# The causal mask of the forgetting attention: from a TensorE matmul to the added row of sums

## The reference

```python
def block(args):
    qi, ci, pi = args
    s = jnp.einsum('bqhd,bkhd->bhqk', qi, k).astype(jnp.float32) * scale
    s = s + ci.transpose(0, 2, 1)[..., None] - cum_k
    mask = kpos[None, :] <= pi[:, None]
    s = jnp.where(mask[None, None], s, NEG_INF)
    p = jax.nn.softmax(s, axis=-1).astype(v.dtype)
    return jnp.einsum('bhqk,bkhd->bqhd', p, v)
```

## Time and profile before

| | us |
|---|---|
| median of 3 runs | 2692.89 |
| lowest and highest | 2692.72, 2695.39 |
| the profiled execution | 2693.89 |
| its span in the profile | 2692.2 |
| TensorE matmuls, busy | 2624.7 (97%) |
| VectorE, busy | 1806.2 (67%) |
| ScalarE, busy | 1130.0 (42%) |
| steps of the forgetting attention | from 1360.5 to about 1977 |

### The profile page before, as it was taken

One profiled execution on the slowest core, in us unless ns is written; L12 is line 12 of the kernel. 1 busy time (PEld: TensorE's weight loads), 2 busy tenths in 40 slices (PEclk: granted clock), 3 DMA queues, 4 the chain that ended last, 5 costly groups with the idle time before them and its releaser, 6 DMA issues.

```text
span 2692.2 us, 39002 instructions
## 1 busy us (share of the span) xinstructions
PE 2624.7 (97%) x12209; PEld 2156.0 (80%) x12209; DVE 1806.2 (67%) x2975; ACT 1130.0 (42%) x2079; POOL 229.9 (9%) x273
## 2 busy tenths in 40 slices
PE   5999999999999999999989999999999999999998
PEld 3688887787888888888868888888878888888886
DVE  7766668785668888888876666666685455644446
ACT  6433336333335555555554444444453322334220
POOL 0000000112120000000001111111100000014100
PEclk9999999999999999999999999999999999999999
DMA  9556864567664444444555545445485455456642
GB/s 359 182 199 204 234 190 122 135 167 163 163 141 119 116 119 116 120 122 123 186 141 130 114 116 130 111 109 108 111 237 159 149 181 184 155 157 195 202 149 101
DMA packets 324800, 418.53 MB, mean 155 GB/s; under 512 B 20392, under 2 KB 223208, under 8 KB 321008
## 3 DMA queue, kind: packets, MB, share of 16 engines
q1 hardware_dynamic: 282048, 343.04, 40.6%
q0 software_dynamic: 29616, 66.12, 13.3%
q10 hardware_dynamic: 13056, 8.39, 1.1%
HBM read 297.90 MB, written 119.59 MB: 155 GB/s over the span
## 4 chain that ended last, share of the span: by engine, by line
PE 87%; DVE 5%; DMA 3%; ACT 3%; issue 2%; SPq 1%; ACTq 0%; DVEq 0%
PE pA L1863 18%; PE pC L1863 18%; PE pD L1863 17%; PE yP L2555 12%; PE zP L2611 11%; PE tP L1765 2%; PE zP L2630 2%; PE sP L2018 2%; PE oP L2041 1%; DMA b_lo<-b_scratch 1%; PE sP L1831 1%; DVE w_lo L1286 1%; DMA w_raw<-in_w_in_dram 1%; PE oP L2043 1%; PE sP L1960 1%
## 5 line engine op out<-in xcount | busy, mean ns | idle before, releaser
L1286 DVE TENSOR_TENSOR w_lo<-w_sum,w_hi 128x512 fp32r<-128x512 f32 x336 | 229.6, 688 | 167.5 <-ACT w_hi L858 166.3
L1863 PE MATMUL pC<-b_hi,w_hi 128*128 128x512 f32 x784 | 308.8, 394 | 6.2 <-DVE b_lo L1260 3.6
L1863 PE MATMUL pA<-b_hi,w_hi 128*128 128x512 f32 x784 | 308.3, 393 | 3.6 <-ACT ctile L874 1.3
L1863 PE MATMUL pD<-b_hi,w_hi 128*128 128x512 f32 x784 | 307.5, 392 | 2.4 <-DVE b_lo L1482 1.3
L1863 PE MATMUL pC<-b_hi,w_lo 128*128 128x512 f32 x784 | 307.1, 392 | 0.0
L1863 PE MATMUL pA<-b_hi,w_lo 128*128 128x512 f32 x784 | 306.9, 392 | 0.0
L1863 PE MATMUL pA<-b_lo,w_hi 128*128 128x512 f32 x784 | 306.7, 391 | 0.0
L1863 PE MATMUL pD<-b_hi,w_lo 128*128 128x512 f32 x784 | 306.1, 390 | 0.0
L1863 PE MATMUL pC<-b_lo,w_hi 128*128 128x512 f32 x784 | 306.1, 390 | 0.0
L1863 PE MATMUL pD<-b_lo,w_hi 128*128 128x512 f32 x784 | 306.0, 390 | 0.0
L180 ACT CAST w_hi<-w_raw 128x1024 fp32r<-128x1024 f32 x122 | 128.5, 1054 | 354.0 <-PE zP L2611 175.2
(11 more groups left out here) (303 smaller groups left out, 5098.6 us busy)
## 6 DMA issues: line engine op xcount, KB each, us to landing
w_raw<-in_w_in_dram SPq DMA_DIRECT2D x168, 512.0 KB, 5.8
proj_scratch<-ctile SPq DMA_DIRECT2D x168, 256.0 KB, 2.2
proj_scratch<-ctile POOLq DMA_DIRECT2D x168, 256.0 KB, 6.0
bg_raw<-in_w_ada_dram SPq DMA_DIRECT2D x64, 512.0 KB, 4.6
w_raw<-in_w_out_dram SPq DMA_DIRECT2D x58, 512.0 KB, 4.0
w_raw<-in_w_br_swa_dram SPq DMA_DIRECT2D x32, 512.0 KB, 4.1
w_raw<-in_w_br_fox_dram SPq DMA_DIRECT2D x32, 512.0 KB, 3.9
aux<-proj_scratch SPq DMA_DIRECT2D x64, 256.0 KB, 4.0
```

The source lines that it names most:

```text
L1286: nc.vector.tensor_tensor(ring(k, True), factor(k), ring(k, False).bitcast(F32), ALU.subtract).then_inc(in_lo, 1)
L1863: last = nc.tensor.matmul(bank(r, k)[:], w[:, j, :], b[:, j, :], start=(k < 4 and n == 0), stop=(n == 11), skip_group_check=True)
```

## The change

The mask matmul and its two constant operands `ident_r` and `mask_r` are dropped. The constant mask stays as float32 (`mask_f`). Before the minimum of step i, VectorE adds the mask to block i of `c_cols`, so that the row that is added to the scores holds the mask. From step i + 1 on that block has to be free of it: ScalarE keeps a copy of each block in `c_kept` before VectorE changes it, and puts it back behind the exponential of the step. A new semaphore `c_block` orders the two: odd values for a kept block, even ones for a masked one. ScalarE instead of VectorE now waits for the load of `c_cols`. Two semaphores of the start, `c_one` and `c_padded`, become one, `c_ready`. The diff, cut to its core:

```diff
@@ main_gpsimd
                 own(nc.gpsimd.memset(mask_f[:], 0.0))
-                own(nc.gpsimd.affine_select(out=mask_f[:], in_=mask_f[:], compare_op=ALU.is_ge,
-                                            fill=-NEG, base=0, pattern=[[-1, P]], channel_multiplier=1))
-                own(nc.gpsimd.tensor_copy(mask_r[:], mask_f[:]))
-                pool.wait_ge(ident_ready, 1)
-                nc.gpsimd.tensor_copy(ident_r[:], ident[:]).then_inc(consts, 1)
+                nc.gpsimd.affine_select(out=mask_f[:], in_=mask_f[:], compare_op=ALU.is_ge, fill=-NEG, base=0,
+                                        pattern=[[-1, P]], channel_multiplier=1).then_inc(consts, 1)
@@ main_scalar, head
+                    def keep(i):
+                        nc.scalar.copy(c_kept[:, i % 2, :], c_cols[:, i * P:(i + 1) * P]).then_inc(c_block, 1)
+
+                    act.wait_ge(c_cols_loaded, 16 * h + 16)
+                    keep(0)
                     for i in range(8):
                         if i < 7:
                             q_high(i + 1)
                         exponentials(i)
+                        if i < 7:
+                            nc.scalar.copy(c_cols[:, i * P:(i + 1) * P], c_kept[:, i % 2, :])
+                            keep(i + 1)
@@ main_vector, head
                     for i in range(8):
+                        diagonal = c_cols[:, i * P:(i + 1) * P]
+                        dve.wait_ge(c_block, 16 * h + (2 * i + 1))
+                        nc.vector.tensor_tensor(diagonal, diagonal, mask_f[:], ALU.add).then_inc(c_block, 1)
+                        dve.wait_ge(c_block, 16 * h + (2 * i + 2))
                         dve.wait_ge(f_qk, 8 * h + (i + 2))
-                        if i == 0:
-                            dve.wait_ge(c_cols_loaded, 16 * h + 16)
@@ main_tensor, scores
                                 last = nc.tensor.matmul(dst, fq[:], fk[:, c0:c1], start=(part == 0), stop=(part == 2))
-                                if part == 0 and a == i // 4:
-                                    nc.tensor.matmul(sP[:, a, (i % 4) * P:(i % 4 + 1) * P], ident_r[:], mask_r[:],
-                                                     start=False, stop=False)
```

More of the change, by code:

```diff
@@ L274, in build @@
             ident = sb("ident", [P, P], F32, main)
-            ident_r = sb("ident_r", [P, P], F32R, main)
-            mask_r = sb("mask_r", [P, P], F32R, main)
+            mask_f = sb("mask_f", [P, P], F32, main)
             c_cols = sb("c_cols", [P, SEQ], F32, main)
@@ L299, in build @@
                     sm = sb("sm", [P, 4, 5], F32, s00)
-                    mask_f = sb("mask_f", [P, P], F32, s00)
                 with ExitStack() as s01:
@@ L342, in build @@
                 fo_st = sb("fo_st", [P, 2, P], F32, s3)
+                c_kept = sb("c_kept", [P, 2, P], F32, s3)
             og_in = [sem(f"og_in_{q}") for q in range(5)]
@@ L352, in build @@
             xh_copied = sem("xh_copied")
-            c_one = sem("c_one")
-            c_padded = sem("c_padded")
+            c_ready = sem("c_ready")
+            c_block = sem("c_block")
             c_loaded = sem("c_loaded")
@@ L1202, in main_vector @@
                 nc.vector.memset(halves[P // 2:P, 1:2], 1.0)
-                nc.vector.memset(c_sb[:, KD:KD + 1], 1.0).then_inc(c_one, 1)
+                nc.vector.memset(c_sb[:, KD:KD + 1], 1.0).then_inc(c_ready, 1)
                 def x_stat(t):
@@ L1405, in main_vector @@
                 dve.wait_ge(c_loaded, 32)
-                nc.vector.tensor_copy(c_pad[:, :, 0], c_sb[:, 0:KD]).then_inc(c_padded, 1)
+                nc.vector.tensor_copy(c_pad[:, :, 0], c_sb[:, 0:KD]).then_inc(c_ready, 1)
                 dve.wait_ge(ada_b_ready, 1)
@@ L1770, in main_tensor @@
                                     ).then_inc(ada_b_turned, 1)
-                pe.wait_ge(c_one, 1)
+                pe.wait_ge(c_ready, 1)
                 def turn_x(t):
@@ L1789, in ada_multiply @@
                         pe.wait_ge(xt_copied, 16)
-                    pe.wait_ge(c_padded, 1)
+                    pe.wait_ge(c_ready, 2)
                     pe.wait_ge(ada_loaded[slot], 32 * (r // 4 + 1))
```

## The result

The changed kernel takes **2708.8 us** (median of 6 runs, 2707.4 to 2711.2) against 2693.4 of the kernel before on the same chip (2692.6 to 2695.4). The ratio is 1.0055, with a 95% interval of 1.0046 to 1.0065: **15.4 us slower**. The forecast was 2699, with a range up to 2703; the time lies outside.

The account below looks back on a forecast made before the run. TensorE was taken to set the pace, with no engine having slack around step 5. Terms -7.0 + 7.2 + 3.2 + 2.4 + 0.3 = +6.1 us gave 2699 us from the median 2692.89, range 2693 to 2703.

Parts of the forecast that it names:

- rival (d): ScalarE's copies don't overlap: 0.19 x 8 at step 5, +1.5 us, 2700.5; chance 0.17 together with Rival (c).
- The matmuls' 0.11: TensorE: each of 64 removed mask matmuls saves its 0.11 us step, 7.0 us in all.
- Added to VectorE: 64 additions of 128x128 ahead of the maxima put each maximum 0.35 to 0.40 us later, taken as 0.36.
- The w_raw load: Heads 1 to 6: additions of steps 2 and 3 delay the next weights' load; +3.2 us, between nothing and 6.3.
- 0.3 for the last: Last head: behind step 7, ScalarE's output projection work hangs on the last maximum, and one mask is lost; +0.3 us.
- Rival (c): The clock falls in head 0 as its wait grows to 2.8 us: +1.6, 2701; chance 0.17 together with rival (d).
- Head 0: Additions and copies delay VectorE's already late weights at steps 1 and 2, and the load; +2.4 us.
- 0.9 of step 5: Step 5, each head: 0.79 us more wait for the copy of pC plus 0.11 for its mask matmul; +7.2 over eight.
- Rival (a): The load lands by itself and is no wait, so 3.2 and 0.6 drop out: +2.3 us, 2695; chance 0.30.
- (b): ScalarE and VectorE have room, so TensorE just gets shorter: -7.0 us, 2686; chance 0.03.

Follow-up runs that it names:

- both_kept: Kernel before with its mask matmuls kept, plus VectorE operations of the addition's size and the change's two ScalarE copies per step; 2705.1 us against 2693.8.
- adds_23: nomask with VectorE's addition of zeros back in steps 2 and 3 of each head alone; 2695.1 us against 2694.0 of the kernel before.
- adds_5: nomask with VectorE's addition of zeros back in step 5 of each head alone; 2695.9 us against 2694.0 of the kernel before.
- nomask_copies: nomask with the ScalarE copies back and no additions; 2692.9 us against 2694.0 of the kernel before.
- adds_rest: nomask with VectorE's addition of zeros back in steps 0, 1, 4, 6 and 7 of each head; 2690.5 us against 2694.0 of the kernel before.
- nomask: Changed kernel without its 64 additions and 120 ScalarE copies, mask matmuls out too, so no causal mask; 2688.9 us against 2694.0 of the kernel before.
- stall_5: nomask with two plain ScalarE copies in step 5 ahead of the copy of pC, and the fv_raw load held back; 2701.5 us against 2693.8 before.

## Why the prediction was wrong, point by point

**Right: what bounds, and where.** TensorE's wait in pC at step 5 was to grow from 0.27 to between 1.4 and 1.7 us in the looped heads; it grew to 2.0 to 2.2, in that place and in no other of those heads. The copies overlap as the nearest row had it: 0.39 for two against 0.43 forecast, so rival (d) is not borne out. The Trainium skill (VectorE: DVE Perf Modes, The TRN2 errata — SBUF-src ops pay a fixed extra latency per instruction) has the bubble exposed between instructions, by my estimate 0.29 us a copy; the trace has that length, 0.28 to 0.29, but the copies start 0.19 to 0.20 us apart. The matmuls' 0.11 is borne out by the period, 0.85 for eight. That four masks of a head beside the longer chain save nothing was right as well: the period of `both_kept` is 0.4 longer than the changed kernel's, which is the other four.

**Step "Added to VectorE": 0.36, measured 0.44 to 0.48.** The addition itself lasts 0.28 as forecast. The register instruction of the looped heads, for which I allowed some hundredths, carries the wait for the addition's end and holds VectorE 0.15 us: 7.4 us in 48 times in the waits view. In head 0, where the memset itself has the wait, the maximum starts 0.33 behind the addition's start. That is 0.1 per addition, and three of them count.

**Step "The w_raw load": 0.20 + 0.33 per head, measured 0.95.** The table of times from one matmul gives the change at step 5: fpT 0.95 later than before, the maximum another 0.46, the copy of pC another 0.40, together 1.81 (4.42 to 6.23). My terms for the same three were 0.53 (and 0.11 for step 5's own matmul), 0.36 and 0.43, together 1.43. The mechanism was the right one. Its size was not: I let the load land 0.72 later, with the masks of steps 2 to 5 1.16; w_sum came 1.46 later (-3.02 to -1.56), since each addition was longer and the load's end followed its start in full. I had also let a part of it vanish in VectorE's wait of 0.43 ahead of w_lo; that room was used up and all beyond it, 1.0, was passed on. `adds_23` and `adds_5` show the two halves apart. In this frame it is 0.4 us a head. From head 0's pC wait to the last pA wait the changed kernel took 10.3 more, 5.4 without the falls, where my terms gave 3.6 (six heads of 0.9 + 0.53 - 0.88, and 0.3 for the last): 1.8 more.

**Rival (c) named the wrong place.** I priced a fall of the clock in head 0 alone, where the wait at step 1 was to grow to 2.8. It grew to 2.42, and the clock stayed at 1.00 behind it (in `nomask_copies` and `adds_rest` it did fall there, behind 2.09 and 2.00). The falls came behind the pC waits of the looped heads, three of 1.6 us, 4.9 us in all. I had the row of a fall behind 3.5 us and my own forecast of waits of 1.4 to 1.7 in seven more heads, with no row in between, and did not put the two together. At waits of 1.4 to 1.7 the later traces show no fall, so this step hangs on the one before: the wait had been put too short. In the profiled execution it is the largest part of the miss.

**Head 0: +2.4, measured more.** Up to its pC wait it took 3.8 us more; my terms were 2.4 and 0.9 of step 5, less 0.66 for six matmuls, 2.6. A wait of 1.93 at step 0, where the kernel before has none, is in it (0.88 in `nomask`), and 0.78 instead of 0.44 at step 2. The kernels differ here by up to 3 us for no reason that I can name (59.9 us in `nomask`, 62.7 in `nomask_copies`, with a clock of 0.87 instead of 0.96 in 1340 to 1380), so I don't split it up further.

**Together.** The profiled execution grew by 17.3, 11.2 more than 6.1. Of these are 1.8 load and addition, 4.9 clock, 1.2 head 0, and 3.2 lie ahead of and behind the attention and are not put down to the change. By medians the miss is 9.3; the median execution has no trace, so it can't be split up in the same way. Rival (a), the load as no wait, was given 0.30 and is contradicted by the issue and start times; (b) too. The upper bound that I gave to the load's term, 3.1 above its value, and three falls would have carried the range to 2707, still short of 2708.8.

## What to carry to other kernels

Work that is put in front of a step of a chain without slack is paid at that step and again through whatever that step triggers: here a buffer's release, a load and the sums behind it brought two earlier additions undiminished to the same wait. Before moving work off the bounding engine, look for the idle time of the receiving engine and put it there: with the mask matmuls gone, the same 64 additions and 120 copies cost 15.4 us in one order and left a gain of 3.6 in another. And when a wait of TensorE grows to about 2 us, ask for the clock behind it: here six of ten waits of 1.8 us and more brought 1.6 us on top.

## What the runs showed of the hardware

- A wait in pC of 1.8 to 2.2 us was followed in six cases of ten by some 3 us at a granted clock of 0.5 (the 1.2 GHz level): 11 matmuls in 4 us instead of 21, 1.6 us lost. None of 101 shorter ones was. It happened also where nothing but ScalarE copies made the wait (1.89 in `stall_5`).
- A wait for the end of VectorE's own last instruction, put into a register instruction in a looped head, holds VectorE 0.15 us (48 times in the changed kernel, 7.4 us). The register wait for something long done costs nothing that shows: in `nomask_copies` the maximum of step 5 starts 2.61 us behind the last matmul of the scores, as in `nomask`.
- Two ScalarE copies of 128x128 start 0.19 to 0.20 us apart, and last 0.28 to 0.29.
- The load of w_raw, two DMAs of 512 KB, took as long when it was issued 0.96 us later: from issue to landing the second took 7.92 us in `nomask` and 7.88 in `adds_23` (head 3).
